# Parts of two weight tiles moved ahead of the two inversion bursts, in TensorE's order of a mixed gated-delta, gated-linear and sparse-attention kernel

## The reference

```python
p = x @ w_in                                    # q, k, v, gate and two logits
qkv = causal_conv_silu(p[..., :GDN_QKV], conv_w)
...
diff = gc[..., :, None] - gc[..., None, :]
decay = jnp.where(causal, jnp.exp(jnp.where(causal, diff, 0.0)), 0.0)
kb = k * beta
A = jnp.where(strict, jnp.einsum('bhncd,bhnsd->bhncs', kb, k) * decay, 0.0)
...
uw = lax.linalg.triangular_solve(A + eye, rhs, left_side=True, lower=True, unit_diagonal=True)
...
def step(S, inp):
    v_new = u_n - jnp.einsum('bhcd,bhde->bhce', w_n, S)
    o = jnp.einsum('bhcd,bhde->bhce', qd_n, S) + jnp.einsum('bhcs,bhse->bhce', qk_n, v_new)
    S = S * gl_n[..., None, None] + jnp.einsum('bhcd,bhce->bhde', kd_n, v_new)
    return S, o
```

## Time and profile before

| | |
|---|---|
| median of 3 runs | 3542.06 us (3540.57 to 3542.14) |
| the profiled execution | 3533.72 us |
| its span, first to last instruction | 3532.0 us |
| mean granted TensorE clock | 0.977 |
| TensorE busy | 3338.2 us, 95% |
| DVE, ScalarE, POOL busy | 1619.6, 1115.5, 458.2 us |

### The profile page before, as it was taken

How to read it: one execution, slowest core, us unless ns; L and a number is a source line. 1 busy time by engine, 2 the same in 40 slices (tenths; PEclk the granted TensorE clock), 3 DMA queues, 4 the chain that set the end, 5 groups by cost and what they waited for, 6 DMA issues and landing times.

```text
span 3532.0 us, 46767 instructions
## 1 busy us (share of the span) xinstructions
PE 3338.2 (95%) x19373; PEld 2546.6 (72%) x19373; DVE 1619.6 (46%) x3386; ACT 1115.5 (32%) x2259; POOL 458.2 (13%) x729
## 2 busy tenths in 40 slices
PE   8899999998999989999999999999999999999997
PEld 6775876677587657757747788778844688888886
DVE  3533444343334444543553799576621333333234
ACT  4441342244234323403443222466601311111112
POOL 0210111021001251302252122000000000000000
PEclk9999999999999999999999999999999999999999
DMA  2110100111010101101112132100040111111111
GB/s 99 73 37 12 42 19 25 30 31 37 6 43 19 43 15 42 49 6 42 60 42 88 36 105 87 48 1 37 17 187 0 42 48 48 48 48 48 48 48 48
DMA packets 40047, 159.64 MB, mean 45 GB/s; under 512 B 5271, under 2 KB 9977, under 8 KB 34330
## 3 DMA queue, kind: packets, MB, share of 16 engines
q1 hardware_dynamic: 39834, 156.65, 13.1%
HBM read 136.71 MB, written 19.92 MB: 44 GB/s over the span
## 4 chain that ended last, share of the span: by engine, by line
PE 85%; DVE 6%; ACT 4%; POOL 2%; issue 2%; DMA 1%; SPq 0%; POOLq 0%; DVEq 0%; ACTq 0%
PE pp L553 10%; PE pp L555 10%; PE pp L554 10%; PE pp L1188 7%; PE pp L1190 7%; PE pp L1189 7%; PE pp L723 5%; PE pp L1170 3%; PE pp L1160 3%; PE pp L876 3%; PE pp L1127 2%; PE pp L1111 2%; PE pp L653 1%; PE pp L667 1%; PE pp L683 1%
## 5 line engine op out<-in xcount | busy, mean ns | idle before, releaser
L553 PE MATMUL pp<-gx_hi,pw_hi 128*128 128x512 f32 x1584 | 650.9, 411 | 29.9 <-DVE pw_lo L1787 29.0
L555 PE MATMUL pp<-gx_hi,pw_lo 128*128 128x512 f32 x1584 | 628.7, 397 | 0.0
L554 PE MATMUL pp<-gx_lo,pw_hi 128*128 128x512 f32 x1584 | 628.2, 397 | 0.0
L553 PEld LDWEIGHTS pp<-gx_hi,pw_hi 128*128 128x128 f32 x1584 | 304.1, 192 | 102.5 <-DVE pw_lo L1787 32.2
L555 PEld LDWEIGHTS pp<-gx_hi,pw_lo 128*128 128x128 f32 x1584 | 303.6, 192 | 67.0
L554 PEld LDWEIGHTS pp<-gx_lo,pw_hi 128*128 128x128 f32 x1584 | 304.2, 192 | 59.0
L1188 PE MATMUL pp<-x_hi,wt_hi 128*128 128x512 f32 x704 | 274.1, 389 | 1.1 <-DVE x_lo L2372 1.1
L1189 PE MATMUL pp<-x_lo,wt_hi 128*128 128x512 f32 x704 | 273.9, 389 | 0.0
L1190 PE MATMUL pp<-x_hi,wt_lo 128*128 128x512 f32 x704 | 273.9, 389 | 0.0
L723 PE MATMUL pp<-xT,arena 128*128 128x512 f32 x512 | 233.8, 593 | 6.3 <-DVE arena L1963 6.3
L1787 DVE TENSOR_TENSOR pw_lo<-arena,pw_hi 128x1024 fp32r<-128x1024 f32 x73 | 89.6, 1229 | 239.5 <-ACT pw_hi L1243 239.5
(11 more groups left out here) (436 smaller groups left out, 6007.8 us busy)
## 6 DMA issues: line engine op xcount, KB each, us to landing
arena<-in_tiles_dram SPq DMA_DIRECT2D x73, 512.0 KB, 3.5
arena<-in_units_dram SPq DMA_DIRECT2D x33, 1024.0 KB, 4.8
xT<-in_tiles_dram SPq DMA_DIRECT2D x27, 512.0 KB, 3.8
xT<-in_w_outs_dram SPq DMA_DIRECT2D x6, 2048.0 KB, 8.5
arena<-gates_scratch SPq DMA_DIRECT2D x16, 512.0 KB, 4.5
gates_scratch<-arena SPq DMA_DIRECT2D x11, 512.0 KB, 5.1
arena<-in_xT_dram SPq DMA_DIRECT2D x8, 512.0 KB, 8.5
y<-in_x_dram SPq DMA_DIRECT2D x1, 4096.0 KB, 14.3
```

The lines of the kernel that those rows point to most:

```text
L553: mm(b[:, hs], wh[:, c], X[0][:, k, hs], k == 0, False)
L554: mm(b[:, hs], wh[:, c], X[1][:, k, hs], False, False)
L555: m = mm(b[:, hs], wl[:, c], X[0][:, k, hs], False, k == 7)
```

## The change

`gdn_order` gets two numbers, `early` and `late`, which are 0 for all engines but TensorE, where both are 2. The generator of tiles 9 to 11 is made before burst 0 and `early` of its twelve steps are run ahead of it. Between the bursts the interleave takes 12 - early - late steps through `paced`, and what is left of the tiles is run after the last chunk's steps and ahead of burst 1.

```diff
+        def paced(steps, n):
+            for _ in range(n):
+                next(steps)
+                yield
+
-        def gdn_order(g, tiles, decay, tee, before_scan, scan_step):
+        def gdn_order(g, tiles, decay, tee, before_scan, scan_step, early=0, late=0):
...
             interleave([four(0), v_steps])
+            gates = tiles(g, range(9, 12), True)
+            for _ in range(early):
+                next(gates)
             tee(g, 0)
-            interleave([four(1), tiles(g, range(9, 12), True)])
+            interleave([four(1), paced(gates, 12 - early - late)])
+            run(gates)
             tee(g, 1)
...
-                gdn_order(g, tiles, decay, tee, before_scan, scan_step)
+                gdn_order(g, tiles, decay, tee, before_scan, scan_step, 2, 2)
```

## The result

The changed kernel takes 3554.24 us (median of 6, 3550.61 to 3556.35), the kernel before 3542.1 (3540.57 to 3548.11). The ratio is 1.0034, 95% interval 1.0022 to 1.0046: slower by 12 us, where 3538.5 was forecast and at most 3549.

What follows compares the result with a forecast made beforehand. TensorE, working 95% of the span, was taken as the bound; -3.2 (first burst), +0.6 (later stretch) and +1.7 (low clock) gave -0.9 us a group, -3.6 in all: 3538.5 us, range 3529 to 3549.

Steps and rivals of the forecast that it cites:

- First burst: 15 tile-9 matmuls moved between the last value tile's transpose and the first inversion burst: gain 3.2 us a group.
- three cases of the prediction's first part: Clock around the moved matmuls: full, gain 4.2 us; one 3.4 us low stretch, 3.2; low for 6.8 us, 1.8.
- Between the bursts: Up to chunk 6's transpose: 9 more matmuls cost 2.07 us, one stall of 1.88 us goes; net 0.2 us later.
- The last chunk: Chunk 6's to chunk 7's transpose: no matmuls cover the chain through other engines; 7.48 us, TensorE idle over 5 us.
- Behind it: Chunk 7's transpose to second burst: 33 matmuls, 7.88 us at full clock, plus 1.7 us for low clock after the stall.
- Sum: All terms together: -3.2 + 0.6 + 1.7 = -0.9 us a group, -3.6 us over four groups, 3538.5 us.
- second and third part: From burst 0 to burst 1: +0.2 us to chunk 6's transpose, +0.4 us from there to the second burst.
- sentence in brackets: On the last chunk: counts 144 - 15 matmuls left; the moved ones' 3.44 us credited in the first part, paid here.
- Slower, because the low clock lasts: Rival: each gap is followed by 6.8 us of low clock; +2.2 us a group, four +8.8, 3550.9 us; chance 0.13.
- Faster, because the clock holds: Rival: clock holds at both places, -3.6 us a group, 3527.7 us; at only one, 3533; chance 0.27 together.
- A second stall: Rival: chunk 6 also waits for its chain, by 3 us a group; +8.4 us over four groups, 3550.5; chance 0.02.
- The signs of being wrong: Chunk 6 to 7 chain not 7.5 us, clock not low behind it, or burst at full clock no faster than now.

Runs made afterwards that it cites:

- filled stall: Changed kernel plus 15 useless 128x512 matmuls per group ahead of chunk 7's transpose, where TensorE waits: 3542.7 us, ratio 1.0001 against the kernel before.
- early half alone: Changed kernel with early 2, late 0, so only the matmuls ahead of the first burst are moved: 3526.45 us, ratio 0.9947 against the kernel before.
- split kernel: Early 2, late 0, with 6 of the 15 matmuls ahead of chunk 3's transpose and 9 behind it: 3520.37 us, ratio 0.9946 against the kernel before.
- the gate behind in the kernel before: Kernel before, with only ScalarE's gate of tile 10 moved behind chunk 7's copies: 3541.14 us, ratio 0.9999 against the kernel before.

## Why the prediction was wrong

The mechanisms were read rightly, and the sum was made wrongly. Point by point:

- *First burst.* Forecast: one low stretch of 3.4 us, the burst 0.2 us later in effect. Measured: that in three groups, the clock held in group 0, and the end of burst 0 at -0.1 us a group ((8.3 - 8.6) / 4). The three cases of the prediction's first part were the right ones and two of them occurred.
- *Between the bursts.* Forecast +0.2 to chunk 6's transpose; measured +0.1 to +0.2 in three groups and +1.7 in group 2, +0.5 on average. Chunk 5's stall of 1.7 us went as said. A low stretch behind burst 0, which two groups of before have as well, came in three; the sum had no term for it.
- *The last chunk.* Forecast 7.48 us; measured 7.50 in all four groups. The idle 4.13 and 1.43 us were foreseen.
- *Behind it.* Forecast 7.88 at full clock and 1.7 for a low stretch of 3.4 us, 9.6; measured 9.49, 10.48, 10.47 and 10.42. In three groups the low clock covered 5.3 us of the matmuls and not 3.4, which is 0.9 us a group more. The filled stall shows the whole of it: 7.85 when the clock holds.
- *Sum.* **This is the step that failed.** The first part gave "Gain 3.44 - 0.2 = 3.2 us", where the 3.44 us are matmuls that the later stretch no longer has to do. The second and third part then measured the later stretch with 129 matmuls in it, not 144: +0.2 and +0.4 are already the difference after the 15 have left. The sentence in brackets there says that they are "credited in the first part and paid in this one"; they were credited in both. Without the second credit a group is +0.2 + 0.6 + 1.7 = +2.5 us, four are +10, and the time is 3552.1, 2 us from the one measured. With the longer low stretch it is +3.2 a group against +3.3. That it comes so close is partly luck: the first term is 0.3 us a group too high and the second 0.3 too low, each by the clock in one group of four.
- *What it hid.* By that false credit the late half looked harmless, and so did the whole. The experiments say otherwise: the early half alone is -17 us, and taking two steps more out of the interleave turns this into +12.
- *Rivals.* "Slower, because the low clock lasts" had the right sign and part of the cause, for 0.13; its own sum carried the same error, and with it the range ended at 3549. "Faster, because the clock holds" is what the early half alone does by another way: its gain is the cover of two gaps, and the clock adds to it only in some groups. "A second stall" did not come: chunk 6's transpose has no wait in any group.
- *The signs of being wrong.* None of the three was met: the chain took 7.5 us, the clock was low behind it, and the burst at full clock was faster. They watched the mechanisms, and nothing watched the sum.

The Trainium skill, page TensorE: Matmul & The Clock Gate, section What's actually happening, has the low clock as the default that activity releases. The trace agrees: 0.50 behind the stall of the changed kernel, 1.00 when 15 useless matmuls fill it.

## What to carry to other kernels

Work that is moved out of a stretch is worth its length once. Count a stretch either by what leaves it or by its new end, and check the sum by adding up all stretches with the work each now holds. An interleave that hides a chain on other engines needs, in each turn, as much work as that chain is long: read the chain's length from the engine that runs it without waiting, and take filler from the turns that have more than enough (here perhaps chunks 4 and 5; no run tried it), never the last from one turn. TensorE's idle time costs twice when it is long: here a stall of 4.1 us cost 1.6 to 2.8 us more in the clock behind it, eight times in eight; one of 2.4 us cost 1.6 more in two groups of four, and one of 1.5 us nothing in four. (Ahead of the first and the third stand 1.4 us idle for POOL and some small products, ahead of the second matmuls.) Behind the 1.9 us ahead of chunk 3's transpose, with the 15 matmuls following at once, the clock fell in some groups and not in others of one and the same kernel; why is open.

## What the runs showed that I had not expected

- TensorE's instructions seem to be held up by a big transfer. A burst has over five hundred small matmuls, and while the 2 MB of output weights moved, TensorE stood idle with no wait that the profile shows. A row of the kernel with the filled stall:

```profile
542.71 0.27 PE L678 MATMUL pp<-arena 64*64 64x64 f32 x1 [2.07 <-issue]
```

The window behind it, at a granted clock of 0.68; the clock fell after this gap as well, and the burst took 22.4 us:

```profile
543.50:548.00 4.50, 4.50 (x116) 4.50 (x114) 1.97 (x5) 1.11 (x4) 1.27 (x1) 0.68 0.02 4
```

Every burst 1 of the kernel before has one such gap of 1.1 to 1.8 us, and every one of the changed kernel one of 1.6 to 1.7.

In the changed kernel's DMA view of 540 to 552 us the queue that carries instructions has two transfers beside those of the weights:

```profile
q1 hardware_dynamic: 144, 2.10, 48.2%
q8 instruction: 2, 0.03, 1.1%
```

Held back until the burst was over, the transfer left no such gap: 18.40 us four times in place of 20.2 to 20.3. That the instructions come late because of the transfer is the reading that fits; the runs show only that the gaps go with it.
- A faster clock doesn't help a burst whose start another engine sets. In the split kernel burst 0 started 2.9 us after the transpose and took 19.7 us; with the early part alone, where the clock held, it started at 3.8 and took 18.8, and both ended 22.6 us after the transpose.
- One kernel's executions spread more than I had assumed for two of the edits: the gate behind in the kernel before ran from 3529 to 3546 us. The stretches that an edit acts on, measured in the traces, told them apart better than two medians.
